# A decoder layer on one core: first tokens rounded by VectorE, two matmuls and two squares moved, one weight split earlier, token factor taken into the last product's operand

## The reference, cut to what matters

```python
h = rms_norm(x, norm1_g)
proj = h @ w_in                      # q, k, v, pool input, two gates
a = rms_norm(diff_attention(q, k, v, lam), subln_g) * (1 - lam_init)
p = causal_pool_mixer(xp, pool_w, pool_scale)
merged = g0 * (a @ w_up_attn) + g1 * (p @ w_up_pool)      # g = sigmoid(proj gates + b)
x = x + merged @ w_o
h2 = rms_norm(x, norm2_g)
u = square(relu(h2 @ w_mlp_in))
y = x + u @ w_mlp_out
```

## Time and profile before

| what | value |
|---|---|
| median of three runs | 1232.14 us (1232.0 to 1232.17) |
| the profiled execution, its own time | 1231.99 us |
| its span | 1230.2 us |
| PE busy | 1222.3 us (99%), granted clock 0.9 or more in all 40 slices |
| weight loads (PEld) busy | 1009.8 us (82%) |
| DVE busy | 980.3 us (80%) |
| ACT busy | 573.5 us (47%) |
| POOL busy | 106.9 us (9%) |
| DMA | 181.82 MB, 148 GB/s over the span |

### The profile page before, as it was taken

One profiled execution on the slowest core, in us unless ns is written; L12 is line 12 of the kernel. 1 busy time (PEld: TensorE's weight loads), 2 busy tenths in 40 slices (PEclk: granted clock), 3 DMA queues, 4 the chain that ended last, 5 costly groups with the idle time before them and its releaser, 6 DMA issues.

```text
span 1230.2 us, 16093 instructions
## 1 busy us (share of the span) xinstructions
PE 1222.3 (99%) x5766; PEld 1009.8 (82%) x5766; DVE 980.3 (80%) x1397; ACT 573.5 (47%) x981; POOL 106.9 (9%) x157
## 2 busy tenths in 40 slices
PE   9999999999999999999999999999999999999998
PEld 7878888888888888888888888888888888888887
DVE  6857876778997687854698787878879988879798
ACT  7546666666644324323465454544554333333330
POOL 1122232324100050000000000000000000000000
PEclk9999999999999999999999999999999999999999
DMA  9201111013474556412425556565389554263233
GB/s 369 81 18 35 54 51 35 18 46 110 168 243 163 175 172 226 137 49 89 129 94 188 174 203 215 179 239 177 132 299 361 185 184 143 86 237 103 103 103 137
DMA packets 119583, 181.82 MB, mean 148 GB/s; under 512 B 7120, under 2 KB 57168, under 8 KB 119504
## 3 DMA queue, kind: packets, MB, share of 16 engines
q1 hardware_dynamic: 119360, 180.79, 42.8%
q10 hardware_dynamic: 144, 0.00, 0.0%
HBM read 126.24 MB, written 54.53 MB: 147 GB/s over the span
## 4 chain that ended last, share of the span: by engine, by line
PE 94%; DVE 2%; ACT 1%; DMA 1%; issue 1%; SPq 0%; POOL 0%; ACTq 0%; POOLq 0%
PE bank L2527 85%; PE bank L2702 2%; PE bank L2657 2%; PE bank L2636 2%; PE bank L2594 1%; DMA x_tile<-in_x 1%; PE bank L2585 1%; DVE slot_lo L1614 1%; DVE small L1704 1%; ACT prob L1141 0%; ACT slot_hi L1076 0%; PE bank L2661 0%; SPq L619 0%; DVE wT_lo L1687 0%; DVE sum L1923 0%
## 5 line engine op out<-in xcount | busy, mean ns | idle before, releaser
L2527 PE MATMUL bank<-s_lo,o_hi 128*128 128x512 f32 (+1 forms) x452 | 175.0, 387 | 0.0
L2527 PE MATMUL bank<-s_hi,o_hi 128*128 128x512 f32 (+1 forms) x452 | 175.0, 387 | 0.0
L2527 PE MATMUL bank<-s_hi,o_lo 128*128 128x512 f32 (+1 forms) x260 | 100.3, 386 | 0.0
L2527 PE MATMUL bank<-featT_hi,pair_hi 128*128 128x512 f32 x256 | 99.6, 389 | 0.0
L2527 PE MATMUL bank<-featT_hi,pair_lo 128*128 128x512 f32 x256 | 99.6, 389 | 0.0
L2527 PE MATMUL bank<-featT_lo,pair_hi 128*128 128x512 f32 x256 | 99.6, 389 | 0.0
L2527 PEld LDWEIGHTS bank<-s_lo,o_hi 128*128 128x128 f32 x452 | 84.9, 188 | 17.4
L2527 PEld LDWEIGHTS bank<-s_hi,o_hi 128*128 128x128 f32 x452 | 84.9, 188 | 17.4
L1573 ACT ACTIVATE s_hi<-s_raw 128x2048 fp32r<-128x2048 f32 x28 | 53.7, 1918 | 93.8 <-DMA s_raw<-u_store 93.7
L1549 ACT ACTIVATE c<-c 128x512 f32<-128x512 f32 x64 | 40.0, 624 | 123.1 <-DVE c L2371 123.1
L2371 DVE TENSOR_TENSOR c<-bank,c 128x512 f32<-128x512 f32 x112 | 75.6, 688 | 22.2 <-PE bank L2527 19.3
(11 more groups left out here) (283 smaller groups left out, 3160.5 us busy)
## 6 DMA issues: line engine op xcount, KB each, us to landing
s_raw<-u_store SPq DMA_DIRECT2D x28, 1024.0 KB, 5.6
pair_raw<-in_w_mlp_in SPq DMA_DIRECT2D x16, 1024.0 KB, 6.1
u_store<-s_tile SPq DMA_DIRECT2D x64, 256.0 KB, 2.1
o_raw<-in_w_mlp_out SPq DMA_DIRECT2D x16, 1024.0 KB, 8.2
u_store<-u_tile SPq DMA_DIRECT2D x48, 256.0 KB, 2.4
gate_store<-out_tile SPq DMA_DIRECT2D x32, 256.0 KB, 2.1
gate_raw<-in_w_in SPq DMA_DIRECT2D x8, 1024.0 KB, 5.4
front<-in_v_and_high SPq DMA_DIRECT2D x8, 512.0 KB, 7.9
```

The source lines that it names most:

```text
L2527: mm = nc.tensor.matmul(out, a, b, start=start and i == 0, stop=stop and i == len(steps) - 1, skip_group_check=onto)
```

## The change

- ACT no longer runs `plain_hi_part(0)`; DVE computes that tile itself (`first_hi_part`, a multiplication by the column of norm1_g), ahead of its other work. Ten matmuls on ones become nine.
- `spread_rstd(0)` moves on PE from behind round (1, 4) to behind round (1, 5). On ACT, `x_square(4)` and `x_square(5)` move from behind the first h_hi parts to ahead of `spread_copy(0)`; squares 6 and 7 follow h_hi 0 and 1.
- DVE runs `late_rest(5)` one step earlier, between two side sums instead of behind the second.
- The token factor of the last product goes into its operand: `scale_last_s` multiplies s (128x2048) by the factor before ACT rounds it, which now waits for that; `scale_c11(t)` multiplies the four accumulator tiles, one behind each of the products 22 to 25; `last_add` only adds.

```diff
@@ ACT
             for k in range(KD):
                 v_w_hi(k)
-                plain_hi_part(k)
+                if k > 0:
+                    plain_hi_part(k)
                 if 1 < k < 6:
                     x_square(k - 2)
+            x_square(4)
+            x_square(5)
             spread_copy(0)
             for k in range(KD):
                 h_hi_part(0, k)
-                if k < 4:
-                    x_square(4 + k)
+                if k < 2:
+                    x_square(6 + k)
                 elif k == 4:
                     v_hi_part(7)
@@ down_hi(n)
-                act.wait_ge(s_in[n % 3], 16 * (n // 3 + 1))
+                if n == DOWN - 1:
+                    act.wait_ge(s_scaled, 1)
+                else:
+                    act.wait_ge(s_in[n % 3], 16 * (n // 3 + 1))
@@ DVE
+            def first_hi_part():
+
+                dve.wait_ge(front_in[0], 16)
+                nc.vector.tensor_scalar(featT[0][:, 0, HIGH], front[0][:, HIGH], g1_col[:, 0:1], None,
+                                        ALU.mult).then_inc(first_hi, 1)
...
-                        if LATE_ROWS[p - 4] == g:
+                        if LATE_ROWS[p - 4] == g and p != 5:
                             late_rest(p)
@@ behind weights_lo, ahead of the second side_add
+                    if g == ROWS + 1:
+                        late_rest(5)
...
             dve.wait_ge(vec_in, 16)
+            first_hi_part()
...
+            def scale_last_s():
+
+                n = DOWN - 1
+                dve.wait_ge(inverse_ready, 4)
+                dve.wait_ge(s_in[n % 3], 16 * (n // 3 + 1))
+                s = s_raw[n % 3]
+                nc.vector.tensor_tensor(s[:], s[:], mean[0][:].unsqueeze(1).to_broadcast([P, 4, HT]),
+                                        ALU.mult).then_inc(s_scaled, 1)
+
+            def scale_c11(t):
+
+                dve.wait_ge(inverse_ready, 4)
+                dve.wait_ge(d_added, 4 * (DOWN - 7) + t + 1)
+                part = acc[:, t, LOW]
+                nc.vector.tensor_tensor(part, part, mean[0][:], ALU.mult).then_inc(c11_scaled, 1)
@@ last_add(i)
+                dve.wait_ge(c11_scaled, t + 1)
                 dve.wait_ge(d_tile, 4 * (DOWN - 1) + i + 1)
-                nc.vector.tensor_tensor(part, part, bank[:, last_bank(i), cols], ALU.add).then_inc(last_added, 1)
-                dve.wait_ge(last_added, i + 1)
-                nc.vector.tensor_tensor(part, part, mean[0][:, cols], ALU.mult).then_inc(y_ready, 1)
+                nc.vector.tensor_tensor(part, part, bank[:, last_bank(i), cols], ALU.add).then_inc(y_ready, 1)
@@ loop over the products
                 down_add(n, 0)
                 down_add(n, 1)
-                if n + 2 < DOWN:
+                if n + 2 == DOWN - 1:
+                    scale_last_s()
+                if n + 2 < DOWN and n + 2 != DOWN - 1:
                     down_lo_s(n + 2)
                 if n < DOWN - 2:
                     down_add(n, 2)
                     down_add(n, 3)
+                if n + 2 == DOWN - 1:
+                    down_lo_s(n + 2)
+                if DOWN - 7 < n < DOWN - 2:
+                    scale_c11(n - DOWN + 6)
@@ PE
-            for i in range(10):
+            for i in range(9):
                 nc.tensor.matmul(bank[:, v_bank(0), :], ones[:, 0:P].bitcast(F32R), ones[:].bitcast(F32R), start=True, stop=True)
...
-                if k == 4:
+                if k == 5:
                     spread_rstd(0)
```

More of the change, by code:

```diff
@@ L271, in trunk_layer @@
         diag_ready, spread_full, spread_ready = sem("diag_ready"), sem("spread_full"), sem("spread_ready")
+        first_hi = sem("first_hi")
         x_squared, x_mean, x_inv, plain_hi, plain_split, h_ready, h_hi, h_split = (sem(n) for n in (
@@ L306, in trunk_layer @@
             "t_f", "t_hi", "t_ready", "p_done", "first_copied", "up_sum", "relu_done", "u_ready", "s_ready"))
-        o_f, d_hi, d_lo, d_tile, d_added, v_moved, folded, last_added, out_scaled, y_ready = (sem(n) for n in (
-            "o_f", "d_hi", "d_lo", "d_tile", "d_added", "v_moved", "folded", "last_added", "out_scaled", "y_ready"))
+        s_scaled, c11_scaled = sem("s_scaled"), sem("c11_scaled")
+        o_f, d_hi, d_lo, d_tile, d_added, v_moved, folded, out_scaled, y_ready = (sem(n) for n in (
+            "o_f", "d_hi", "d_lo", "d_tile", "d_added", "v_moved", "folded", "out_scaled", "y_ready"))
         def wait(eng, s, value):
@@ L1087, in plain_hi_part @@
                 act.wait_ge(front_in[k], 16)
-                if k == 0:
+                if k == 1:
                     act.wait_ge(vec_in, 16)
@@ L1615, in split_lo @@
                                         ALU.subtract).then_inc(w_ready, 1)
+            def first_hi_part():
+                dve.wait_ge(front_in[0], 16)
+                nc.vector.tensor_scalar(featT[0][:, 0, HIGH], front[0][:, HIGH], g1_col[:, 0:1], None,
+                                        ALU.mult).then_inc(first_hi, 1)
             def plain_lo_part(k):
-                dve.wait_ge(plain_hi, k + 1)
+                if k == 0:
+                    dve.wait_ge(first_hi, 1)
+                else:
+                    dve.wait_ge(plain_hi, k)
                 nc.vector.scalar_tensor_tensor(featT[1][:, k, HIGH], front[k][:, HIGH], g1_col[:, k:k + 1],
@@ L2695, in v_round @@
                     if half == 1:
-                        pe.wait_ge((plain_hi, plain_split, v_w_ready)[i], k + 1)
                         if i == 0:
+                            pe.wait_ge(*((first_hi, 1) if k == 0 else (plain_hi, k)))
                             pe.wait_ge(v_w_rounded, k + 1)
+                        else:
+                            pe.wait_ge((plain_split, v_w_ready)[i - 1], k + 1)
                     elif i < 2:
```

## The result

The changed kernel takes **1233.69 us**, the median of 20 runs (1233.04 to 1235.58), against 1232.12 (1231.84 to 1232.87) for the kernel before in as many runs on the same chip: ratio 1.0016, 95% interval 1.001 to 1.0022. Forecast were 1232.0 and a range of 1230.2 to 1233.0; the result lies above it. The 20 runs lie in two groups, 1233.04 to 1233.80 (eleven) and 1234.34 to 1235.58 (nine). The profiled execution (1233.41, span 1231.6) is of the lower one, 1.42 above that of the kernel before.

What follows compares the result with a forecast made beforehand. PE was taken to bound the kernel (94% of the span). Start -0.1, late tile +0.3 and end -0.05 made 0.15 us gained: 1231.84 by the profiled 1231.99, 1232.0 as median, range 1230.2 to 1233.0.

Steps and rivals of the forecast that it cites:

- First tile and nine matmuls: PE's start: with DVE making the first tile and nine matmuls on ones, first round at 5.31 instead of 5.89, 0.58 gained.
- The term for its slow start: PE's first round: 0.15 us added to the usual 2.72 of a round, putting the first spread at 21.78.
- The squares and DVE's chain: Start: square 5 delays the spread copy to 23.66 and DVE's first norm part to 24.29, 2.10 late.
- the hold of one lo part: DVE at the start: an operation on two SBUF tiles meeting POOL's second product waits for its end, 0.85 us.
- The step that failed: DVE's thirteen operations from first norm part to v_lo_part(7): start at 34.2, square 7 at 27.2, second spread at 35.0.
- the term of the start: Second spread at 35.0 against 34.99 before, a waiting spread costing 0.1 more: start's gain given back, -0.1 us.
- slower start: Rival: POOL holds two DVE operations, v_lo_part(7) ends at 35.8, PE loses 1.0 at the start; 1233.5 us, chance 0.11.
- What stands behind the late chain: Low half's norm parts and values' lo parts, 0.6 us later on DVE: costed at nothing, up to 0.6 without cover.
- The late tile: PE's weight load near 308: late_lo wait of 0.90 gone, 0.85 gained, 0.3 left after gate products; bounds 0 and 0.85.
- G7 and G3: Gate products near 336 and 339: PE waits for DVE's operands, leaving 0.49 of the 0.85 after G7, 0.3 after G3.
- DVE's later work moves by 0.27: Late tile: DVE's work behind late_rest(5) shifts by 0.27 us, because it idles from 305.34 to 305.61.
- The term for the queue: Kernel's end: y ready 0.46 sooner, but last stores queue, landing 1229.8 to 1230.2; -0.05 taken, bounds +0.46 and -0.4.

Runs made afterwards that it cites:

- experiment 6: Kernel before with the start's edits except the first tile by DVE and with ten matmuls on ones, late tile and token factor undone: median 1232.95 us.
- experiment 1: Kernel before with the start's edits alone (first tile by DVE, nine matmuls on ones, later first spread, squares ahead of its copy): median 1233.26 us, ratio 1.0012.
- experiment 5: Changed kernel with squares 4 to 7 put back behind the first four h_hi parts, the spread left behind round 5: median 1232.95 us.
- experiment 4: Kernel before with the token factor's edits alone and one 512 KB store left out (rows y[7] not written): median 1231.77 us.
- experiment 7: Changed kernel with the second spread one round later too, behind round (0, 2): median 1231.81 us.
- experiment 8: Changed kernel with the second product with the identity on ACT, as four 128x128 multiplications, in place of POOL's 128x512: median 1232.72 us.
- experiment 13: Changed kernel without the token factor's edits, second spread behind round (0, 2), second product with the identity on ACT: median 1231.10 us, ratio to kernel before 0.9991.
- experiment 10: Changed kernel with the 1 MB load of pair_raw issued ahead of the 256 KB load of res: median 1234.36 us.
- experiment 2: Kernel before with the late tile's move alone (late_rest(5) between the side sums): median 1231.70 us, ratio 0.9996.
- experiment 3: Kernel before with the token factor's edits alone: median 1232.51 us, ratio 1.0002.
- experiment 9: Kernel before with the start's edits alone, plus ten matmuls of a zero tile filling PE's stand ahead of the second spread: median 1234.81 us.

## Why the prediction was wrong, point by point

**First tile and nine matmuls.** The first round starts at 5.32 (5.31 forecast). The term for its slow start was mis-sized: 0.15 was taken, 8.48 - 5.32 - 2.72 = 0.44 was measured. So 0.28 is gained by round 2, not 0.58, and the spread is at 22.08, not 21.78. The term is no fixed size: it is 0.12 to 1.05 in the twelve profiles with nine matmuls on ones and 0.14 to 0.49 in the five with ten. That the tenth had taken up slow time may be a part of it, but is not shown. It made no difference (experiment 6).

**The squares and DVE's chain.** The copy at 23.58 (23.66), the first norm part at 24.19 (24.29) and the hold of one lo part, 1.53 us beside POOL's product, came as forecast. **The step that failed is the one from there to v_lo_part(7), and with it the term of the start: -0.1 in the sum, -1.15 measured (experiment 1).** It took square 7 at 27.2, with x tile 7's landing at 26.5 as before. The tile landed at 27.7, the square ran from 27.75, and the h_hi part behind it came at 28.81; DVE's 0.90 of waiting for it was not reckoned with. v_lo_part(7) starts at 34.78, not at 34.2, and the second spread at 35.67, not at 35.0. The 0.58 by which the square is later than the end of the h_hi ahead of it (26.55 + 0.62 = 27.17) is as much as v_lo_part(7) is late. That is read from the trace; no run has the changed order with the tile landed at 26.5, and with the squares back (experiment 5) the chain is as late by another route. The rival "slower start" had place and rule right, one for one from 34.95, but its cause wrong (no second operation was held), and its chance of 0.11 was too low: I had written down that the time hangs on landings, and then kept them fixed. Beside these 0.7 us the start's edits cost 0.3 at 295 and a drift of 0.2, for neither of which there was a term.

**What stands behind the late chain** was costed at nothing, and nothing was found there.

**A stand I priced by its length only.** I forecast 1.4 us of waiting ahead of the second spread as neutral, since before PE started it at the same time. But before, PE had worked up to it. Now it stood 1.5 to 2.0 us, and in 12 of 32 runs of the changed kernel the time was above 1234.3; the one such profile shows the lower clock behind the stand, 1.6 us. The difference of the median from the lower group is this. The Trainium skill (TensorE: Matmul & The Clock Gate, Part 1: The HAM clock gate) says of a kernel's start that the number of slow matmuls differs between runs of one kernel, since the monitor runs free of it. The traces agree for the start: the first round of the changed kernel is longer than 2.72 by 0.12 to 0.61 in its four profiles. Whether the same holds for the fall behind a stand no run here shows.

**The late tile.** The wait went nearly as forecast (0.91 gained, 0.85 forecast), and 0.2 net were left in the changed kernel, 0.42 when alone, against 0.3. The giving back was put in the wrong place: 0.55 at G7 and G3, where only G3's 0.18 was found. "DVE's later work moves by 0.27" was right, and who waits for it was not followed: the attention row's output sum at 310.08, ACT's chain behind it, the copy that frees a bank, PE at 312 and 315.

**The token factor.** DVE's end came as forecast (last out_scale at 1225.67, less PE's 0.98 is 1224.69; forecast 1224.7), and the last add stays behind PE, 1228.23. The term for the queue was taken at its fast end, -0.05. It measures -0.44 in the trace and -0.40 alone, the slow bound. The mechanism is shown by experiment 4. The price per store was right and the overlap that I counted on was not there: the store of 512 KB leaves at 1225.70 and lands 2.7 later, at 1228.4, and the last of the 1024 KB behind it lands at 1231.2, 2.8 later, the slow end of my 2.4 to 2.8.

**In no term:** the 0.3 at 295.

**The sum.** The three parts alone give +1.15, -0.42 and +0.40, together +1.13, or 1233.25, the middle of the lower group. Measured is a loss of 1.57 at the median where a gain of 0.15 was forecast; the start takes most of the difference, and the rest of it above 1233.25 is the upper group, nine of the 20 runs.

## What to carry to other kernels

An engine's earlier start is worth what the chain behind it can follow: look for the next wait of that engine and ask whether the work that ends it moved as well; here PE came 1.1 us earlier to a value that came later. A moved wait is better met by giving the waiting engine other work than by speeding up what stands ahead of it: here the second spread a round later took 1.9 off the median (experiment 7), the product moved to ACT 1.0, and only 0.15 of that at the second spread (experiment 8). When stores move together, count the bytes in the queue ahead of the last one at full price.

## What the runs showed of the hardware that I had not expected

- Early matmuls of 512 columns start 0.43 us apart and later 0.23, and the moment of the change differs between executions: the first group of four takes 1.51 us in the changed kernel and 2.01 in that of experiment 13 (both from 5.3), and the next still 1.22 there, while the granted clock reads 1.00 in both.
- TensorE's granted clock was 0.50 to 0.57 for 3 us behind a stand of 1.98 us in one of four profiles of the same program, and 1.00 in the three with stands of 1.51 to 1.64. It was also 1.00 behind one of 1.91 (experiment 10), so the length alone does not decide. The kernels without a stand in experiments 2, 3, 4, 7 and 13 had no run in the upper group (one of 13 is another matter, see the result), and the kernel before had one of 134 at 1234.30. In experiment 9, whose stand is filled, ten of eleven are above 1234.3, but at a mean clock of 1.000.
- One instruction less in ACT's program, 280 us earlier, delayed one of its instructions by 0.28 us, and a dummy in its place undid it. What lies behind it is open.
- x tile 7, issued at 17.2 to 17.5 in nearly all traces, lands at 26.4 to 26.5 in the kernel before and in experiments 2 and 3, and 1.0 to 1.5 us later in all traces with the start's edits, but also in experiment 4, where the start is untouched and where it costs nothing. So it is no sure consequence of the change, and the one value of the trace before was not to be relied on. Why it moves is open, and so is the late landing of pair_raw in experiment 9.
- With the stores close together, SyncE's issue of the last 128 KB takes 0.65 us instead of the 0.33 of the kernel before, and it lands 2.5 us behind the start of its issue instead of 1.7. With one store of 512 KB left out both are nearly back, 0.33 and 1.8 (experiment 4).
